# The first block's 24 gate panels as six groups of seven block products

## The reference, cut to what matters

```
h = rmsnorm(x, attn_norm_g)                       # 512 tokens x 1024
z = h @ w_in                                      # mixers A, B and C (differential attention)
gates = sigmoid(h @ w_gate + b_gate)              # w_gate is 1024 x 3072
...
s = qk^T * scale + bias; p = softmax(s)           # 4 heads, 2 score maps each
a = p[:, 0] - lam * p[:, 1];  o = a @ v
merged = g_a*(y_a @ proj_a) + g_b*(y_b @ proj_b) + g_c*(y_c @ proj_c)
x = x + merged @ w_out
```

## Time and profile before

| what | value |
|---|---|
| median of 3 runs | 1427.68 us (1427.46 to 1429.75) |
| the profiled execution | 1428.33 us, span 1426.6 us, granted clock 0.999 |
| PE busy | 1415.9 us, 99% of the span |
| DVE, ACT, POOL busy | 76%, 53%, 5% |
| chain that ended last | PE 94%, DVE 3%, DMA 1%, issue 1% |
| DMA | 139 GB/s mean over the span |

### The profile page before, as it was taken

How to read it: one execution, slowest core, us unless ns; L and a number is a source line. 1 busy time by engine, 2 the same in 40 slices (tenths; PEclk the granted TensorE clock), 3 DMA queues, 4 the chain that set the end, 5 groups by cost and what they waited for, 6 DMA issues and landing times.

```text
span 1426.6 us, 22475 instructions
## 1 busy us (share of the span) xinstructions
PE 1415.9 (99%) x8561; PEld 1235.3 (87%) x8561; DVE 1084.4 (76%) x1591; ACT 756.8 (53%) x1071; POOL 71.9 (5%) x81
## 2 busy tenths in 40 slices
PE   9999999999999999999999999999999999999997
PEld 7878888888899999999988777878888989899896
DVE  4836675686899699879857776967655897979888
ACT  6215555334666465456734555535434866657474
POOL 0000000000100000000000000000000100000100
PEclk9999999999999999999999999999999999999999
DMA  8722222233556776765243323213212867585851
GB/s 297 244 87 89 92 72 89 89 94 102 174 163 160 223 175 175 198 184 136 79 160 103 117 92 118 75 62 119 72 45 73 242 178 211 151 240 133 241 142 74
DMA packets 56573, 198.64 MB, mean 139 GB/s; under 512 B 6136, under 2 KB 6648, under 8 KB 56228
## 3 DMA queue, kind: packets, MB, share of 16 engines
q1 hardware_dynamic: 43584, 155.47, 32.8%
q0 software_dynamic: 8640, 30.94, 12.2%
q10 hardware_dynamic: 4260, 11.00, 2.4%
HBM read 195.26 MB, written 6.06 MB: 141 GB/s over the span
## 4 chain that ended last, share of the span: by engine, by line
PE 94%; DVE 3%; DMA 1%; issue 1%; ACT 0%; SPq 0%; POOLq 0%; POOL 0%; DVEq 0%; ACTq 0%
PE ps L2045 30%; PE ps L2047 29%; PE ps L2046 29%; PE ps L2209 1%; DMA raw_sum<-down_dram 1%; PE ps L2224 1%; PE ps L3676 1%; PE ps L3576 1%; DVE wl L1642 1%; PE ps L2097 0%; DMA tables<-tables_dram 0%; DVE y L3369 0%; DVE xcl L1774 0%; PE ps L3696 0%; DVE raw_sum L1649 0%
## 5 line engine op out<-in xcount | busy, mean ns | idle before, releaser
L2046 PE MATMUL ps<-hl,wh 128*128 128x512 f32 (+1 forms) x1024 | 351.4, 343 | 0.0
L2045 PE MATMUL ps<-hh,wh 128*128 128x512 f32 (+1 forms) x952 | 337.4, 354 | 0.0
L2047 PE MATMUL ps<-hh,wl 128*128 128x512 f32 (+1 forms) x952 | 331.2, 348 | 0.0
L908 ACT ACTIVATE wh<-stage 128x1024 fp32r<-128x1024 f32 x129 | 136.2, 1058 | 255.2 <-PE ps L2047 247.0
L2046 PEld LDWEIGHTS ps<-hl,wh 128*128 128x128 f32 x1024 | 194.4, 190 | 19.9
L2045 PEld LDWEIGHTS ps<-hh,wh 128*128 128x128 f32 x952 | 180.4, 189 | 26.8 <-issue 4.3
L2047 PEld LDWEIGHTS ps<-hh,wl 128*128 128x128 f32 x952 | 180.3, 189 | 23.4
L1324 DVE TENSOR_TENSOR wl<-stage,wh 128x1024 fp32r<-128x1024 f32 x128 | 156.1, 1221 | 49.1 <-ACT wh L908 48.9
L3256 DVE TENSOR_TENSOR wl<-raw,wh 128x1024 fp32r<-128x1024 f32 x75 | 90.9, 1220 | 20.6 <-ACT wh L2664 20.4
L1642 DVE TENSOR_TENSOR wl<-raw,wh 128x1024 fp32r<-128x1024 f32 (+1 forms) x75 | 88.7, 1187 | 22.4 <-ACT wh L1103 21.9
L2664 ACT ACTIVATE wh<-raw 128x1024 fp32r<-128x1024 f32 x75 | 78.7, 1054 | 50.8 <-PE ps L2047 45.0
(11 more groups left out here) (475 smaller groups left out, 3239.9 us busy)
## 6 DMA issues: line engine op xcount, KB each, us to landing
stage<-stream_dram SPq DMA_DIRECT2D x134, 512.0 KB, 3.6
raw<-up_dram SPq DMA_DIRECT2D x64, 512.0 KB, 7.1
raw<-down_dram SPq DMA_DIRECT2D x52, 512.0 KB, 5.9
raw_sum<-up_dram SPq DMA_DIRECT2D x16, 512.0 KB, 3.9
raw_sum<-up_dram POOLq DMA_DIRECT2D x16, 512.0 KB, 8.3
raw<-up_dram POOLq DMA_DIRECT2D x16, 512.0 KB, 8.9
raw_sum<-down_dram SPq DMA_DIRECT2D x13, 512.0 KB, 4.7
raw_sum<-down_dram POOLq DMA_DIRECT2D x13, 512.0 KB, 7.8
```

The source lines that it names most:

```text
L908: A(parts_of(b, p)[0], b.stage[:, p.stage, :], ACT.Copy).then_inc(s.hi_ready, 1)
L2045: MM(out, wh, xh, start=start, stop=False, skip_group_check=True)
L2046: MM(out, wh, xl, start=False, stop=False, skip_group_check=True)
L2047: return MM(out, wl, xh, start=False, stop=stop, skip_group_check=True)
```

## The change

The 1024 x 3072 gate product is cut into six groups of 512 features. In a group the two halves of the contraction's tile pairs and the two halves of the tokens make 2 x 2 blocks, and seven products of blocks replace eight (Strassen's scheme in Winograd's form). A group is seven panels in the order P1, Q5, P6, Q3, P7, P2, R4; a panel is 4 tile pairs by 2 feature tiles by three matmuls of 256 columns. So there are 42 panels (`GATE_ITEMS`) and 1008 matmuls of 256 columns, in place of 24 panels and 576 matmuls of 512.

- **Input combinations** (`gate_gain`, `gate_difference`, `gate_normalise`, `gate_sum`, `gate_hi`, `gate_rest_of`): ACT and DVE make seven token-side blocks of the normalised x and split each in high part and rest, mostly during the q, k and v panels. They lie where x, `hh` and `hl` lay, so x is loaded again (four DMAs) when the gates are done. Four of the splits (Q3, S3, X12, X22) can only be made after the v panels, inside head 0.
- **Weight sums**: four of the seven weight panels of a group are sums. GpSimd makes them in DRAM by plain and accumulating DMAs, 8 per group, 48 in all, in three rounds of two groups; each round is six steps that wait for one another. SP waits for the level that a panel needs before it loads it.
- **Combining the products**: ACT copies the first product to a second PSUM bank (`gate_seed`) and two more to SBUF (`gate_copy`), DVE subtracts twice (`gate_sub`), ACT takes tanh from PSUM or SBUF (`gate_bank`, `gate_differences`). The row scale is now in the inputs.
- **Heads**: one head per group, in groups 0 to 3. Scores 0 and 1 come before P6, scores 2 and 3 inside Q3 (before its fourth step of eight), transposes 0 and 1 inside P2 (before the seventh), the other two inside R4, and the value products behind R4.

SP loads the gate panels by group and product, and x again at the end:

```diff
+    for row in range(P_GATE, P_PROJ):
+        g, product = gate_item(row)
+        if product in GATE_SUM:
+            sp.wait_ge(s.gate_sums.sem, s.gate_sums.at(256 * (g // 2) + 16 * SUM_LEVEL[product]))
+            source = dram["gate_sums"][g, GATE_SUM[product]]
+        else:
+            source = dram["gates"][g, GATE_BLOCK[product]]
+        sp.wait_ge(s.lo_ready, row - RING + 1)
+        sp.dma_start(b.stage[:, row % RING, :], source).then_inc(s.load[row % RING], 16)
...
+    sp.wait_ge(s.panel_done, P_PROJ)
+    for c in range(4):
+        sp.dma_start(b.x[:, 2 * c:2 * c + 2, :], dram["x"][:, 2 * c:2 * c + 2, :]).then_inc(s.x_in[c], 16)
```

ACT in a group that carries a head, and at the end of group 5:

```diff
+        gate_seed(i)
...
+        AR(b.vh[:], b.v[:, :, P * i:P * i + P], ACT.Copy).then_inc(s.v_hi, 1)
+        hi(Panel(first))
+        gate_copy(i, Q5)
+        hi(Panel(first + 1))
+        if i == 0:
+            gate_hi("X12")
+        exps(i, 0)
+        exps(i, 1)
+        gate_copy(i, P6)
+        hi(Panel(first + 2))
+        if i == 0:
+            gate_hi("X22")
+        exps(i, 2)
+        exps(i, 3)
+        hi(Panel(first + 3))
+        hi(Panel(first + 4))
+        turned(i, (0, 1))
+        gate_bank(i, P2)
+        hi(Panel(first + 5))
+        turned(i, (2, 3))
+        gate_differences(i)
+        hi(Panel(first + 6))
+        gate_bank(i, R4)
...
+        gate_bank(g, P2)
+        hi(Panel(first + 5))
+        gate_differences(g)
+        if g == 5:
+            for h in range(4):
+                act.wait_ge(s.o_normed, h + 1)
+                A(b.ych[:, h, :], b.o[:, h, :], ACT.Copy, scale=b.subln).then_inc(s.yc_hi, 1)
+        hi(Panel(first + 6))
+        gate_bank(g, R4)
```

DVE in a group that carries a head:

```diff
+        lo(Panel(first))
+        dve.wait_ge(s.v_hi, i + 1)
+        V.tensor_tensor(b.vl[:], b.v[:, :, P * i:P * i + P], f32(b.vh[:]), ALU.subtract).then_inc(s.v_ready, 1)
+        dve.wait_ge(s.bias_in, 16 * i + 16)
+        score_pair(i, 0, 0, (b.bias, b.bias))
+        lo(Panel(first + 1))
+        score_pair(i, 1, 0, (b.bias, b.bias))
...
+        lo(Panel(first + 2))
+        for qb in (2, 3):
+            score_pair(i, qb, 0, (b.bias, b.bias))
...
+        gate_sub(i, Q3)
+        blend(i)
+        gate_sub(i, P7)
+        lo(Panel(first + 3))
+        turned_rest(i, (0, 1))
+        lo(Panel(first + 4))
+        turned_rest(i, (2, 3))
+        lo(Panel(first + 5))
+        lo(Panel(first + 6))
+        head_out(i)
```

POOL, one round of sums, and PE's places for the head:

```diff
+        for g in groups:
+            copied(g, 0, dram["gates"][g, 0])
+            copied(g, 3, dram["gates"][g, 1])
+        summed(16 * pair + 4)
+        for g in groups:
+            added(g, 0, 1)
+            added(g, 3, 2)
+        summed(16 * pair + 8)
+        for g in groups:
+            copied(g, 1, dram["gate_sums"][g, 0])
+        summed(16 * pair + 10)
...
+    for g in range(GATE_GROUPS):
+        if g < 4:
+            between = {P6: {0: [sc(g, 0), sc(g, 1)]}, Q3: {3: [sc(g, 2), sc(g, 3)]},
+                       P2: {6: [tn(g, 0), tn(g, 1)]}, R4: {2: [tn(g, 2)], 5: [tn(g, 3)]}}
```

More of the change, by code:

```diff
@@ L782, in block1 @@
         sp.dma_start(b.raw1[:, r, p.half, 0:p.width], weights1(dram, p, r)).then_inc(s.block_in1[p.half][r].sem, 16)
-    for row in range(P_UP // RING * RING, P_UP):
+    for row in range(P_PROJ + 2 * RING, P_UP):
         load_row(row, row - RING)
@@ L983, in scalar_program, with gate_tile @@
+    for u in range(2 * RING):
+        hi(Panel(P_Q + u + RING))
+        if u < RING:
+            gate_gain(2 * u)
+            gate_gain(2 * u + 1)
+        elif u == 6:
+            gate_hi("X11")
+        elif u == 7:
+            gate_hi("S1")
     for u in range(4):
         hi(Panel(P_V + u + RING))
+        if u == 0:
+            gate_hi("S2")
+            gate_move("X12")
+            gate_move("X22")
     act.wait_ge(s.lines_out, 32)
[L989 to L992, removed]
+    def gate_tile(n):
+        return b.ga[:, n, :] if n < 16 else b.gatec[:, n - 16, :]
@@ new lines, in tanh, with gate_bank, gate_differences @@
+    def tanh(dst, source, n):
+        return AR(dst, source, ACT.Tanh, bias=b.half_bg[:, n:n + 1], scale=0.5)
+    def gate_bank(g, product):
+        bank_b, bank_a, _ = GATE_BANKS[g % 2]
+        bank, h = (bank_a, 1) if product == P2 else (bank_b, 0)
+        act.wait_ge(s.panel_done, gate_panel(g, product).index + 1)
+        for n in range(2):
+            ins = tanh(gate_tile(4 * g + n)[:, M * h:M * h + M], b.ps[:, bank, M * n:M * n + M], 4 * g + n)
+        ins.then_inc(s.gated, 1)
+    def gate_differences(g):
+        act.wait_ge(s.evac, E_GATE + 4 * g + 4)
+        for n in range(2):
+            tanh(gate_tile(4 * g + 2 + n), b.tmp[:, n, :], 4 * g + 2 + n).then_inc(s.gated, 1)
@@ L999, in exp_pair, with squares @@
             A(sc, sc, ACT.Exp, bias=b.neg[:, n:n + 1], accum_out=b.sums[:, n:n + 1]).then_inc(s.exped, 1)
[L1001 to L1032, removed]
+    def squares(pair):
         for h in (2 * pair, 2 * pair + 1):
@@ L1952, in gpsimd_program, with summed, copied, added @@
     G.tensor_tensor(b.ln_rs, b.ln_var, b.expo[:, 0:4], ALU.pow).then_inc(s.ln_pow, 1)
+    def summed(count):
+        pool.wait_ge(s.gate_sums.sem, s.gate_sums.at(16 * count))
+    def copied(g, n, source):
+        G.dma_start(dram["gate_sums"][g, n], source).then_inc(s.gate_sums.sem, 16)
+    def added(g, n, r):
+        G.dma_start(dram["gate_sums"][g, n], dram["gates"][g, r], accum_op=ALU.add,
+                    max_dma_last_dim=4 * D).then_inc(s.gate_sums.sem, 16)
+    for pair in range(GATE_GROUPS // 2):
+        groups = (2 * pair, 2 * pair + 1)
+        if pair:
+            summed(16 * pair)
+        for g in groups:
[9 more added lines that the diff above has]
+        summed(16 * pair + 10)
+        for g in groups:
+            added(g, 1, 2)
+        summed(16 * pair + 12)
+        for g in groups:
+            copied(g, 2, dram["gate_sums"][g, 1])
+        summed(16 * pair + 14)
+        for g in groups:
+            added(g, 2, 3)
     pool.wait_ge(s.omean_ready, 1)
```

452 lines of the change are left out of this document (327 added, 125 removed).

## The result

The changed kernel takes 1460.8 us (median of 4 runs, 1455.6 to 1461.5) against 1427.6 for the kernel before: ratio 1.0221, 95% interval 1.0195 to 1.0247. The forecast was 1432.7 with a range to 1446, so the direction was right and the size wrong: +33 us where +5 was expected. The profiled execution has a span of 1458.8 us, before 1426.6.

What follows compares the result with a forecast made beforehand. TensorE, busy in 99% of the span, was taken as the bound. Matmuls -9.6, head waits +11.2 and the wait at the gates' end +3.5 sum to +5.1 us: 1432.7 us, 8-in-10 range 1421 to 1446.

Steps and rivals of the forecast that it cites:

- Matmuls: PE in the gates: 576 matmuls at 0.2267 us replaced by 1008 at 0.120, 9.6 us less.
- The softmax chain: In each head PE waits for DVE's blend before the transposes: 2.4 us in heads 1 to 3, 3.4 in head 0.
- The added 0.6 for transpose 2: In the heads, transpose 2 waits another 0.15 us each for work behind DVE's blend, 0.6 in all.
- Rival 1: Head waits do not come, the chain being at least 2 us shorter than added up: 1418 to 1422 us, 17%.
- rival 2: Half of the waits come: 1424 to 1430 us, 15%.
- The end of the gates: Ahead of the projections PE waits 3.5 us for the last `ycl`, bounds 2 to 5.
- The sums in DRAM: cost nothing: POOL's weight sums take 52 us a round, below the 62 us that stay hidden, so no cost.
- the limit of 62 us: Longest round of weight sums still hidden, from POOL free at 45 us to R4 of group 4's load at 232.
- Rival 3: Weight sums are late once rounds reach 62 us, each us above costing three; 67 gives 1448 us; 18%.
- estimate of 31 us a round: Weight sums in DRAM by the Trainium skill's 2.0 us and bytes / 436e3 per DMA: about 31 us a round.
- So no drop: PE's clock stays 1.00 behind waits of 2.4 to 3.5 us, as in two earlier 2 us windows without a matmul.
- rival 4: PE's clock falls after its waits, costing some 2 us per wait: 1442 us, 2%.

Runs made afterwards that it cites:

- without sums: Changed kernel with none of the 48 sum DMAs; the four summed products load plain gate-weight blocks without waiting (gates' values wrong): 1437.4 us, ratio 1.0065.
- the filled waits: Against the kernel without sums, PE issues unread matmuls, 16 ahead of each head's first transpose and 26 ahead of the projections: 1433.45 us, ratio 1.0037.
- unused sums: Changed kernel where POOL still makes all sums, but the loads take plain blocks and wait for no sum (gates' values wrong): 1444.3 us, ratio 1.0122.
- early sums: Complete changed kernel with 24 independent copies on SP's queue from 36 us and POOL only adding, in three steps a round: 1440.9 us, ratio 1.0083.
- half the rows: Changed kernel, same sum steps and waits, each sum DMA handling 64 of 128 rows, loads taking plain blocks (gates' values wrong): 1438.4 us, ratio 1.0072.

## Why the prediction was wrong, step by step

**Matmuls: right.** One remark in it is off: an eighth of 130.6 us is 16.3, and 9.6 are left, so 41% of that gain is gone and not a third; the sum used 9.6. The distance is 0.12 in the changed kernel, too (119.76 and 119.88 in PE's timeline):
```profile
119.76 0.28 PE L2356 MATMUL ps<-gx_S,wh 128*128 128x256 f32 x1
119.88 0.28 PE L2357 MATMUL ps<-gx_S,wl 128*128 128x256 f32 x1
```
**The softmax chain: right.** Forecast 2.4 us a head and 3.4 in head 0; measured without sums 2.17, 2.16, 2.17 and 3.33. Both sides of it, in head 1 of the changed kernel, on DVE (the rest that waits for ACT, and the blend):
```profile
155.23 1.23 DVE L1485 TENSOR_TENSOR wl<-stage,wh 128x1024 fp32r<-128x1024 f32 x1 [2.59 <-ACT wh L966]
...
162.53 1.94 DVE L1748 SCALAR_TENSOR_TENSOR s<-s,rec 128x128 f32<-128x128 f32 x4
```
The scores start at 148.81. The blend ends 15.7 us later (forecast 15.9), and PE was ready at 164.53 - 2.17 = 162.36, after 13.55 (forecast 13.5). Head 1 before is in the earlier trace rows. The added 0.6 for transpose 2 did not show as a wait of its own. Rival 1 and rival 2, that the waits don't come or come by half, are out.

**The end of the gates: right,** 3.76 us for 3.5.

**"The sums in DRAM: cost nothing": wrong, the largest error, 23.4 us.** The sums were late from group 2 on. Three parts of that step failed. The round was put together from single DMAs and their latency, 52 us, with the other DMA traffic left out. A sum can be made of engine time: in the window 40 to 280 us the software queue, which carries only these 48 DMAs, took
```profile
q0 software_dynamic: 4224, 25.17, 44.1%
```
(packets, MB, share of 16 engines): 0.441 x 240 / 48 = 2.2 us of all sixteen engines for each, 35 us a round. Beside it the other loads of the stage took 0.27 before and, with 42 panels for 24, 0.42 of the engines without sums. 35 us of work in 62 is 0.57, and with 0.42 by others that leaves no reserve (an estimate; the changed kernel measured 0.76 over its longer stage). Second, the limit of 62 us was set by the last sum (R4 of group 4), for which ACT waited 0.71 us only. The waits that cost came earlier, from P6 of groups 2 and 4 and R4 of group 2, which ACT converts four panels ahead, in front of the turned blocks of heads 1 and 3 and of the exponentials of head 2. Third, a queue that works in order passes a wait on: SP behind the sum, ACT behind SP, DVE behind ACT, PE behind DVE. Rival 3 was this case at 18%; its own rule, three us for each us over 62, gives 3 x 13 = 39 us for rounds of 75, on top of +5. Measured were 23.4, clock included; so the price a microsecond was too high, and the case came all the same.

The Trainium skill (DMA: Bandwidth & Descriptors, Anatomy of one DMA) led to an estimate of 31 us a round. Here 75 us was measured, with other traffic beside the sums; its fit is given for one DMA, and no run here times one that has the engines to itself.

**"So no drop" (rival 4, 2%): wrong, 4.0 us without the sums' waits and part of the 23.4 with them.** The argument was that two windows of 2 us without a matmul still read 1.00. Those windows have no matmul in them, and nothing runs that could show what came next. In the kernel without sums the 2 us window in the middle of head 0's wait reads 1.00 as well, and the low clock comes behind it, when PE works again:
```profile
132.00:134.00 2.00, 0.00 (x0) 1.00 0.00 0
134.00:136.00 2.00, 1.17 (x10) 1.00 0.01 4
136.00:138.00 2.00, 2.00 (x14) 0.56 0.23 57
138.00:140.00 2.00, 2.00 (x13) 0.58 0.67 234
140.00:142.00 2.00, 2.00 (x16) 1.00 0.61 234
```
The price set there, 2 us a wait, fits where the clock fell: 4 us at 0.57 is 1.7 us. That it was PE's idleness is shown by the filled waits, which gave the 4.0 us back.

What stays open: which 2.2 us waits cost clock and which not. It is not a matter of the place: heads 1 to 3 wait 2.16 to 2.17 us both without sums and with unused sums, and the low clock stands behind heads 0 and 2 in the one profile and behind 0, 1 and 3 in the other (0.72 in 164 to 170 us, 1.00 in 194 to 200, 0.60 in 224 to 228). Open is also where the 6.9 us of the unused sums go beyond the wait for POOL.

## What to carry to other kernels

Work that is moved to the DMA engines is priced in time of all sixteen engines and added to what the window already carries; where the two come near one, sums like these can be late, and here were; set the deadline by the first in-order queue that stands behind the data, not by the engine that uses it. A wait of two to four us on a TensorE that was otherwise full cost its length and, in three of the five cases without the sums, some 2 us more for the clock; matmuls that nobody reads, issued in the wait, took that second part away. An instruction that depends on another engine does not belong between two links of the chain that PE will wait for.

## What the runs showed of the hardware that was not expected

- With adds of 512 KB from DRAM to DRAM, POOL issued three and then stood 17.3 us before the fourth, with no releaser shown, in the changed kernel and for 17.1 us in the one with early sums; with half the rows all four went out together (54.63, 3.25 us).
- An add costs more engine time than a copy, by estimate. With early sums the software queue carries the 24 adds alone, 28.6% of 240 us: 2.9 us each on all sixteen engines. In the changed kernel adds and copies mixed average 2.2, which leaves about 1.5 for a copy if an add costs the same there. The Trainium skill (Collectives: The Full Stack, The bandwidth ceiling: the fold count and why AG ≠ RS ≠ AR) says of the add in a ReduceScatter that it needs two source reads where a copy needs one. A ratio of some 1.9 fits that and does not prove it, since the queue also counts 144 packets for an add and 32 for a copy here.
- The granted clock behind equal waits of TensorE (2.17 and 2.16 us) was 1.00 once and 0.57 for 4 us the other time, in one execution; in another kernel's execution the two were the other way round.
- In the profiled run of the early sums a 256 KB load on ACT's queue took 10.6 us to land where it took 2.7 us without sums.
